# A four-layer transformer kernel: the activations' tiles start at other byte distances from the weight rings

## The chip, the cores and the metric

The kernel runs on one core of one Trainium2 chip. The metric is the time on the device in microseconds (us), here the median of three runs. Inside the core, TensorE (PE in the profile) multiplies; a matmul instruction streams its moving operand past a stationary operand that a weight load (PEld) has brought in before. VectorE (DVE), ScalarE (ACT) and GpSimd (POOL) do the work on elements, and SyncE (SP) issues DMA transfers.

## The reference

Activations are a 256 x 1024 matrix in float32. Two layers of a first block are followed by two layers of a second one. Cut to what matters:

```python
# first block, twice (layers 0 and 1)
h = rms_norm(x, mix_pre_norm[l])
m = hybrid_mixer(h, w_in[l], ...)          # delta rule, retention and pooling branches, gates, w_out
x = x + rms_norm(m, mix_post_norm[l])
h = rms_norm(x, ffn_pre_norm[l])
x = x + rms_norm(swiglu(h, ffn_gate[l], ffn_up[l], ffn_down[l]), ffn_post_norm[l])   # 1024 -> 2816 -> 1024

# second block, twice (layers 2 and 3)
u = rmsnorm(h, attn_norm[l])
h = h + hybrid_mixer_2(u, pos, w_in[l], ...)    # three attention branches, gates, w_o
u = rmsnorm(h, mlp_norm[l])
h = h + jnp.square(jax.nn.relu(u @ w_up[l])) @ w_down[l]                             # 1024 -> 4096 -> 1024
```

## The kernel before

**Weights.** All weight matrices are cut into 572 chunks of 128 partitions x 1024 float32. SP brings each chunk into one of four slots of `raw`; ACT rounds it into the ring `whi` (float32r, four slots), and DVE (for 54 chunks POOL) writes the remainder `raw - whi` into the ring `wlo`. A slot is 4096 bytes of each partition and a block of 128 columns in it is 512 bytes, so that every block of either ring starts at the same place modulo 512.

**Activations.** They are split in the same way. The normed stream is `hh` (high part, written by ACT in `high`) and `hl` (remainder, written by DVE in `low`, for the first pair of a turned norm by POOL), each 8 tiles of 256 tokens; a tile is 1024 bytes of each partition. The factor of the output projections is `FH` and `FL` (up to 32 tiles, 22 in layers 0 and 1, 32 in layers 2 and 3), which lie in slots 0 to 7 and 8 to 15 of the area. Each product is then three matmuls (`mm3`): high weights by high activations, high by low, low by high, summed in one bank.

**The order of the work.** Each engine's instructions are written out in program order by one function for each engine (`tensor` for PE). A layer has a mixer, where projections of the stream (`project`, `by_token`) and branches are interleaved with many small matmuls of the delta rule or of attention, and then long stretches of nothing but `mm3`:

- `gu` (layers 0 and 1) and `up` (layers 2 and 3): `project`, weights stationary, `hh` and `hl` moving, 256 columns a matmul;
- `down` of layers 2 and 3: `by_rows`, weights stationary, `FH` and `FL` moving, 256 columns a matmul;
- `wout` and `down` of layers 0 and 1: `tokens`, the other way round, `FH` and `FL` stationary, weights moving, 512 columns a matmul.

Before layer 0's and 1's delta rule there are also 16 matmuls of a small weight `SW`: for each of eight k, `SW[:, k, :]` (16 columns) is stationary under `hh[:, k, :]`, and then `SW[:, k, 0:8]` (8 columns) under `hl[:, k, :]`. `SW[:, k, :]` starts 64 bytes after `SW[:, k - 1, :]`.

**Where the tiles lie.** `sb` hands out addresses in the order of its calls, from byte 16640 of each partition. Worked out from the sizes: `whi` starts at 41216 and `wlo` at 57600, both 256 modulo 512. `hh` starts at 88000, `hl` at 96192, `SW` at 105408 and the area (`region`) at 105920, all 448 modulo 512. So `hh`, `hl`, `FH`, `FL` and the branches' factors (`B0H`, `B0L` and so on, in slots of the area) all start 192 bytes after a block of the rings, modulo 512. That is called the distance below. For the 16 matmuls of `SW` the moving tile starts -64 k bytes from the stationary one, modulo 512: at 0, 448, 384, 320, 256, 192, 128 and 64 for k from 0 to 7.

Of the kernel before, what the change touches and what calls it, by code (L numbers as in the profile page):

```python
# [14 lines left out]
P = 128  # L15
# [42 lines left out]
N_PAR = DEPTH * (N_PAR1 + N_PAR2)  # L58
N_SMALL = 64 + 512 + 8


# [132 lines left out]
def pair(t, j):  # L194
    return t[:, 512 * j:512 * j + 512]
# [76 lines left out]
def program(nc, ins, out):  # L272
    with ExitStack() as ctx:
# [63 lines left out]

        def slot_r(name, i, k):
            return sb(name, [P, k, T], F32R, offset=region + 4096 * i)

# [275 lines left out]
        def scalar(a):  # L616
# [47 lines left out]
            def high(norm, j, *ready):  # L664
                if norm in TURNED and j == 0:
                    a.wait_ge(*v_norm.at("first", norm))
                else:
                    a.wait_ge(*ready)
                for k in (2 * j, 2 * j + 1):
                    h = act(hh[:, k, :], xT[:, k, :], AF.Copy, scale=GAIN[norm][:, k:k + 1])  # L670
# [178 lines left out]
            def merge(name, L, j):  # L849

                a.wait_ge(*gated(name, L, 2 * j))
                act(FH[:, 2 * j:2 * j + 2, :], v3(pair(YY, j)), AF.Copy, scale=0.5).then_inc(*a_br.up("sum", L, j))

# [8 lines left out]
            def first(L):  # L862
# [68 lines left out]
                def product(i):  # L931
                    a.wait_ge(*v_ffn.at("product", L, i))
                    a.copy(FH[:, i, :], FT[:, 512 * (i % 4):512 * (i % 4) + T]).then_inc(*a_ffn.up("high", L, i))

# [30 lines left out]
            def second(L):  # L965
# [113 lines left out]
                def mlp_high(m0):  # L1079
                    f = FT[:, 256 * (m0 % 8):256 * (m0 % 8) + 512]  # L1080
                    a.wait_ge(*a_ffn.at("square", L, m0))
                    a.copy(FH[:, m0:m0 + 2, :], v3(f)).then_inc(*a_ffn.up("high", L, m0))

# [45 lines left out]
        def vector(v):  # L1129
# [52 lines left out]
            def low(norm, j):  # L1182
                v.wait_ge(*a_norm.at("high", norm, j))
                for k in (2 * j, 2 * j + 1):
                    x = stt(hl[:, k, :], xT[:, k, :], GAIN[norm][:, k:k + 1], hh[:, k, :].bitcast(F32), OP.mult, OP.subtract)
                x.then_inc(*v_norm.up("low", norm, j))
# [225 lines left out]
            def merge(L, j):  # L1412

                v.wait_ge(*a_br.at("sum", L, j))
                stt(FL[:, 2 * j:2 * j + 2, :], v3(pair(YY, j)), 0.5, FH[:, 2 * j:2 * j + 2, :].bitcast(F32), OP.mult, OP.subtract).then_inc(*v_br.up("merged", L, j))

# [8 lines left out]
            def first(L):  # L1425
# [104 lines left out]
                def ffn_low(i):  # L1530
                    v.wait_ge(*a_ffn.at("high", L, i))
                    tt(FL[:, i, :], f_(i)[:, 0:T], FH[:, i, :].bitcast(F32), OP.subtract).then_inc(*v_ffn.up("low", L, i))

# [53 lines left out]
            def second(L):  # L1587
# [162 lines left out]
                def mlp_low(m0):  # L1750
                    v.wait_ge(*a_ffn.at("high", L, m0))
                    tt(FL[:, m0:m0 + 2, :], v3(f_(m0)), FH[:, m0:m0 + 2, :].bitcast(F32), OP.subtract).then_inc(*v_ffn.up("low", L, m0))

# [31 lines left out]
        def gpsimd(g):  # L1785
# [28 lines left out]
            def low(norm):  # L1814

                g.wait_ge(*a_norm.at("high", norm, 0))
                for k in (0, 1):
                    x = g.tensor_scalar(SQ2[:, (6 + k) * T:(7 + k) * T], xT[:, k, :], GAIN[norm][:, k:k + 1], None, OP.mult)
                x.then_inc(*g_norm.up())
                g.wait_ge(*g_norm.now())  # L1820
                tt(hl[:, 0:2, :], v3(pair(SQ2, 3)), hh[:, 0:2, :].bitcast(F32), OP.subtract).then_inc(*g_norm.up("low", norm))

# [173 lines left out]
        def tensor(e):  # L1996
# [30 lines left out]
            def parts(job, ready, norm):  # L2027

                b, at = job.banks[0], job.first
                fresh(b, leaves(job.name, job.layer, 0))  # L2030
                for m in range(2):
                    e.wait_ge(*wlo_at(at + m))
                for k in range(8):
                    e.wait_ge(*(a_norm.at("high", norm, k // 2) if k else a_norm.at("first", norm)))
                    for m in range(2):
                        i = (at + m) % RING
                        mm(bank[b][:, m * T:(m + 1) * T], whi[:, i, 128 * k:128 * k + 128], hh[:, k, :], (m, k) == (0, 0), False, True)
                        mm(bank[b][:, m * T:(m + 1) * T], wlo[:, i, 128 * k:128 * k + 128], hh[:, k, :], False, False, True)
                for j in range(4):
                    e.wait_ge(*ready(j))  # L2040
                    for m in range(2):
                        for k in (2 * j, 2 * j + 1):
                            x = mm(bank[b][:, m * T:(m + 1) * T], whi[:, (at + m) % RING, 128 * k:128 * k + 128], hl[:, k, :], False, k == 7, True)
                        if j == 3:
                            x.then_inc(*proj.up("used", at + m, also=(job.name, job.layer, 0) if m else None))
# [61 lines left out]
            def by_token(name, L):  # L2107
                job = JOBS[name, L]
                for c in range(4):
                    i = job.first + c  # L2110
                    e.wait_ge(*wlo_at(i))
                    if c == 0:
                        for s in range(2):
                            fresh(job.banks[s], leaves(name, L, s))
                    for j in range(2):
                        k = 2 * c + j
                        wh, wl = whi[:, i % RING, 512 * j:512 * j + 512], wlo[:, i % RING, 512 * j:512 * j + 512]
                        for s in range(2):
                            ps = bank[job.banks[s]][:, :]
                            xh, xl = hh[:, k, 128 * s:128 * s + 128], hl[:, k, 128 * s:128 * s + 128]  # L2120
                            mm(ps, xh, wh, k == 0, False)
                            mm(ps, xl, wh, False, False)
                            x = mm(ps, xh, wl, False, k == 7)
                            if j == 1 and c == 3:
                                x.then_inc(*proj.up(name, L, s, also=("used", i) if s else None))
                            elif j == 1 and s == 1:
                                x.then_inc(*proj.up("used", i))
                    yield

            def tokens(name, L, ready, norm, then):  # L2130
# [6 lines left out]
                def term(k, b):  # L2137
                    i, s, f = job.first + k, 128 * (b // 2), 512 * (b % 2)
                    wh, wl = whi[:, i % RING, f:f + 512], wlo[:, i % RING, f:f + 512]
                    xh, xl = FH[:, k, s:s + 128], FL[:, k, s:s + 128]  # L2140
                    mm(bank[b][:, :], xh, wh, k == 0, False, True)
# [29 lines left out]
            def by_rows(name, L, ready, after=None):  # L2171
# [299 lines left out]
            def first(L):  # L2471
                norm = f"mixpre{L}"
                h = hh, hl, stream_ready(norm)

# [12 lines left out]
                for k in range(8):  # L2487
                    mm(bank[1][0:16, 0:T], SW[:, k, :], hh[:, k, :], k == 0, False, True)
                    x = mm(bank[1][0:8, 0:T], SW[:, k, 0:8], hl[:, k, :], False, k == 7, True)
                x.then_inc(*e_dn.up("abrow", L))  # L2490
# [24 lines left out]
                norm = f"ffnpre{L}"  # L2515
                rest(project("gu", L, hh, hl, stream_ready(norm), lambda: norm_sum(norm), norm=norm))
                tokens("down", L, lambda k: v_ffn.at("low", L, k), f"ffnpost{L}", "mixpre1" if L == 0 else "attn2")

            def second(L):
                norm = f"attn{L}"  # L2520
                h = hh, hl, stream_ready(norm)

# [78 lines left out]
                norm = f"mlp{L}"  # L2601
                rest(project("up", L, hh, hl, stream_ready(norm), lambda: norm_sum(norm)))
                by_rows("down", L, lambda k: v_ffn.at("low", L, k // 2 * 2), post("last") if L == 3 else None)
# [243 lines left out]
```

## Time and profile before

| | us |
|---|---|
| median of three runs | 1875.36 |
| lowest and highest of them | 1869.99, 1878.12 |
| span of the profiled execution | 1875.1 |
| PE busy in it | 1841.3 (98%), 15964 matmuls |
| DVE, ACT, POOL busy | 1259.6, 956.6, 307.3 |
| HBM read | 305.00 MB, 163 GB/s over the span |

Matmuls are pipelined: the profile gives each its own length of some 0.28 us, while the next one starts some 0.11 us after it. How fast PE gets through a stretch is therefore read from the starts, or from the chain of waits, which gives a stretch's time and its count of instructions. The profile's clock row gives the TensorE clock granted in tenths of full speed (2.4 GHz).

### The profile page before, as it was taken

What the parts mean: (1) busy time and instruction counts of PE and PEld (TensorE: products, weight loads), DVE (VectorE), ACT (ScalarE), POOL (GpSimd) and SP (SyncE); (2) the same over time, 40 slices, a digit from 0 to 9 for tenths busy, and PEclk for the clock granted to TensorE, in tenths of its full rate; (3) what the DMA queues carried; (4) which work ended last, traced back from release to release, by engine and by line L of the source; (5) the groups of instructions that cost most, each with busy time, mean ns of one, the idle gap of its engine ahead of it and who ended that gap; (6) DMA issues with size and microseconds to landing.
All of it is one profiled execution on the core that took longest, in us unless ns stands there. A gap on an engine that the chain in (4) does not pass through costs nothing.

```text
span 1875.1 us, 37406 instructions
## 1 busy us (share of the span) xinstructions
PE 1841.3 (98%) x15964; PEld 1750.7 (93%) x15964; DVE 1259.6 (67%) x1676; ACT 956.6 (51%) x1381; POOL 307.3 (16%) x176
## 2 busy tenths in 40 slices
PE   7999999999999999999999999999999999999998
PEld 7989998998888999999989999999999899999998
DVE  6884677665689557777648865676547785577643
ACT  5634466444563445554545455565434445555533
POOL 0050221000003212200002542310002352230000
PEclk9999999999999999999999999999999999999999
DMA  6443354656445334555656553456555663446652
GB/s 238 157 159 113 125 169 158 214 184 196 154 145 172 113 123 149 178 194 181 204 189 196 193 170 126 147 182 198 185 189 181 206 195 126 136 158 203 189 187 96
DMA packets 92165, 317.66 MB, mean 169 GB/s; under 512 B 11744, under 2 KB 12896, under 8 KB 91744
## 3 DMA queue, kind: packets, MB, share of 16 engines
q1 hardware_dynamic: 91424, 314.69, 51.7%
q8 instruction: 127, 2.08, 0.5%
q10 hardware_dynamic: 576, 0.57, 0.1%
q14 instruction: 38, 0.31, 0.0%
HBM read 305.00 MB, written 1.05 MB: 163 GB/s over the span
## 4 chain that ended last, share of the span: by engine, by line
PE 83%; DVE 12%; ACT 3%; issue 1%; DMA 1%; SPq 0%; DVEq 0%; ACTq 0%
PE bank L2007 82%; DVE wlo L1131 4%; DVE area L1131 3%; DVE area L1137 2%; ACT area L634 1%; ACT whi L640 1%; PE bank L2571 1%; DMA raw<-in_weights 1%; DVE hl L1137 1%; DVE xT L1137 1%; DVE area L1651 0%; DVE area L1649 0%; PE bank L2592 0%; ACT L622 0%; PE bank L2226 0%
## 5 line engine op out<-in xcount | busy, mean ns | idle before, releaser
L1131 DVE TENSOR_TENSOR wlo<-raw,whi 128x1024 fp32r<-128x1024 f32 x518 | 668.6, 1305 | 412.6 <-ACT whi L640 412.3
L2007 PE MATMUL bank<-hh,whi 128*128 128x256 f32 x2928 | 830.0, 284 | 18.5 <-DVE wlo L1131 15.9
L2007 PE MATMUL bank<-hh,wlo 128*128 128x256 f32 x2928 | 814.4, 279 | 0.0
L2007 PE MATMUL bank<-hl,whi 128*128 128x256 f32 x2928 | 807.2, 279 | 0.0
L640 ACT CAST whi<-raw 128x1024 fp32r<-128x1024 f32 x572 | 589.3, 1046 | 398.8 <-PE bank L2007 351.9
L2007 PEld LDWEIGHTS bank<-hh,whi 128*128 128x128 f32 x2928 | 551.3, 188 | 33.8 <-DVE wlo L1131 18.7
L2007 PEld LDWEIGHTS bank<-hl,whi 128*128 128x128 f32 x2928 | 551.1, 190 | 1.4 <-issue 1.4
L2007 PEld LDWEIGHTS bank<-hh,wlo 128*128 128x128 f32 x2928 | 551.4, 188 | 0.0
L1787 POOL TENSOR_TENSOR area<-area 128x512 f32<-128x512 f32 (+4 forms) x86 | 135.1, 1578 | 567.3 <-DVE area L1137 250.6
L1787 POOL TENSOR_TENSOR wlo<-raw,whi 128x1024 fp32r<-128x1024 f32 x54 | 133.9, 2481 | 384.7 <-ACT whi L640 384.7
L2007 PE MATMUL bank<-FH,whi 128*128 128x256 f32 x640 | 180.1, 281 | 0.0
L2007 PE MATMUL bank<-FL,whi 128*128 128x256 f32 x640 | 179.6, 281 | 0.0
L2007 PE MATMUL bank<-FH,wlo 128*128 128x256 f32 x640 | 179.6, 281 | 0.0
L634 ACT ACTIVATE area<-area 128x256 f32<-128x256 f32 (+8 forms) x247 | 140.8, 579 | 45.2 <-DVE area L1137 15.2
L2007 PE MATMUL bank<-area 128*64 128x64 f32 (+6 forms) x2464 | 154.7, 248 | 5.4 <-DVE area L1131 4.7
L2007 PEld LDWEIGHTS bank<-area 128*64 128x64 f32 (+3 forms) x2464 | 133.2, 151 | 24.2 <-issue 6.5
L2007 PEld LDWEIGHTS bank<-FL,whi 128*128 128x128 f32 x640 | 122.3, 191 | 0.1
L2007 PEld LDWEIGHTS bank<-FH,whi 128*128 128x128 f32 x640 | 120.1, 188 | 0.4 <-issue 0.3
L2007 PEld LDWEIGHTS bank<-FH,wlo 128*128 128x128 f32 x640 | 120.5, 188 | 0.0
L1131 DVE TENSOR_TENSOR area<-bank,RSB 128x512 f32<-128x512 f32 (+1 forms) x118 | 80.1, 681 | 37.9 <-PE bank L2007 36.1
L1131 DVE TENSOR_TENSOR area<-bank,area 128x512 f32<-128x512 f32 (+3 forms) x144 | 83.0, 616 | 23.7 <-PE bank L2007 23.3
L2007 PE MATMUL bank<-wlo,FH 128*128 128x512 f32 x240 | 94.9, 395 | 0.0
(132 smaller groups left out, 1907.4 us busy)
## 6 DMA issues: line engine op xcount, KB each, us to landing
raw<-in_weights SPq DMA_DIRECT2D x572, 512.0 KB, 4.0
area<-area SPq DMA_DIRECT2D x96, 64.0 KB, 3.6
area<-area SPq DMA_DIRECT2D x16, 128.0 KB, 3.9
cst<-in_const SPq DMA_DIRECT2D x1, 1188.0 KB, 7.9
cst<-in_const SPq DMA_DIRECT2D x1, 1024.5 KB, 5.6
xT<-in_x SPq DMA_DIRECT2D x4, 256.0 KB, 7.9
out<-xT SPq DMA_DIRECT2D x4, 256.0 KB, 2.9
area<-in_lev SPq DMA_DIRECT2D x2, 384.0 KB, 6.8
```

Of the source, the lines that this page charges most:

```text
L634: return a.activation(dst, src, fn, scale=scale, **more)
L640: a.copy(whi[:, i % RING, :], raw[:, i % RAW, :]).then_inc(*hi.up(i))
L1131: return v.tensor_tensor(dst, x, y, op)
L1137: return v.scalar_tensor_tensor(out=dst, in0=x, scalar=s, in1=y, op0=op0, op1=op1)
L1787: return g.tensor_tensor(dst, x, y, op)
L2007: return e.matmul(ps, x, y, start=start, stop=stop, skip_group_check=skip)
L2571: o = e.transpose(bank[b][:, 128 * u:128 * u + 128], x.grid()[:, j % 2, j // 2, 128 * kb:128 * kb + 128], C("eye"))
```

## The change

The tiles `hh` and `hl` become one pair for each layer, all in the same two places but for a shift under 512 bytes; `FH` and `FL` likewise. The shift sets the distance from a block of the rings to 64, 128, 448 and 224 bytes for the stream of layers 0 to 3, and to 320, 448, 256 and 384 bytes for the factors. All other tiles keep theirs: `RSB`, `SW`, the area and all that lies in it move up by exactly 512 bytes. Each use picks its layer's pair. No instruction is added, removed or moved on any engine, no size changes, and no wait.

For the 16 matmuls of `SW` the distance changes too, since `hh` and `hl` move and `SW` doesn't.

```diff
+STREAM_PHASE = (64, 128, 448, 224)
+
+FACTOR_PHASE = (320, 448, 256, 384)
...
+        whi_at = at[0]
         whi = sb("whi", [P, RING, 1024], F32R)
...
-        hh = sb("hh", [P, 8, T], F32R)
-        hl = sb("hl", [P, 8, T], F32R)
+        stream = at[0]
+        at[0] += 2 * 4 * 8 * T + 512
...
-        def slot_r(name, i, k):
-            return sb(name, [P, k, T], F32R, offset=region + 4096 * i)
+        def slot_r(name, i, k, behind=0):
+            return sb(name, [P, k, T], F32R, offset=region + 4096 * i + behind)
+
+        def from_weights(first, by):
+            return (whi_at + by - first) % 512
+
+        hh, hl = ([sb(f"{name}{L}", [P, 8, T], F32R, offset=stream + 8192 * j + from_weights(stream, STREAM_PHASE[L]))
+                   for L in range(2 * DEPTH)] for j, name in enumerate(("hh", "hl")))
...
-        FH, FL = slot_r("FH", 0, 32), slot_r("FL", 8, 32)
+        FH, FL = ([slot_r(f"{name}{L}", i, 32, from_weights(region, FACTOR_PHASE[L])) for L in range(2 * DEPTH)]
+                  for name, i in (("FH", 0), ("FL", 8)))
...
-                        mm(bank[b][:, m * T:(m + 1) * T], whi[:, i, 128 * k:128 * k + 128], hh[:, k, :], (m, k) == (0, 0), False, True)
+                        mm(bank[b][:, m * T:(m + 1) * T], whi[:, i, 128 * k:128 * k + 128], hh[job.layer][:, k, :], (m, k) == (0, 0), False, True)
...
-                    return mm3(bank[m // 2][:, m % 2 * T:m % 2 * T + T], job.first + k, 128 * m, FH[:, k, :], FL[:, k, :],
+                    return mm3(bank[m // 2][:, m % 2 * T:m % 2 * T + T], job.first + k, 128 * m, FH[L][:, k, :], FL[L][:, k, :],
```

## Rows read from the trace of the kernel before

**Rows 1.** The page: busy time, share and instructions of each engine; granted clock in 40 slices.

```profile
PE 1841.3 (98%) x15964; PEld 1750.7 (93%) x15964; DVE 1259.6 (67%) x1676; ACT 956.6 (51%) x1381; POOL 307.3 (16%) x176
...
PEclk9999999999999999999999999999999999999999
```

**Rows 2.** Chain of waits in seven stretches, 256-column matmuls: start us, us, what, count.

```profile
320.00 110.09 PE bank L2007 x935
...
808.93 39.23 PE bank L2007 x333
...
864.92 54.17 PE bank L2007 x478
...
1252.92 77.11 PE bank L2007 x655
...
1332.97 90.10 PE bank L2007 x765
...
1694.00 76.08 PE bank L2007 x646
...
1774.91 80.21 PE bank L2007 x681
```

**Rows 3.** Groups by shape, PE and PEld, 320 to 430 us: count, busy us, mean ns.

```profile
L2007 PE MATMUL bank<-hl,whi 128*128 128x256 f32 x311 | 87.4, 281 | 0.0
...
L2007 PEld LDWEIGHTS bank<-hl,whi 128*128 128x128 f32 x310 | 59.5, 192 | 0.0
L2007 PEld LDWEIGHTS bank<-hh,whi 128*128 128x128 f32 x311 | 58.4, 188 | 0.0
```

**Rows 4.** The same view, 866 to 918 us.

```profile
L2007 PE MATMUL bank<-hl,whi 128*128 128x256 f32 x154 | 42.5, 276 | 0.0
...
L2007 PEld LDWEIGHTS bank<-hl,whi 128*128 128x128 f32 x153 | 28.7, 188 | 0.0
```

**Rows 5.** Timeline of PE around one interruption: start us, us, engine, what.

```profile
862.49 0.28 PE L2007 MATMUL bank<-hh,wlo 128*128 128x256 f32 x1
862.60 0.37 PE L2007 MATMUL bank<-hh,whi 128*128 128x256 f32 x1
862.81 0.28 PE L2007 MATMUL bank<-hl,whi 128*128 128x256 f32 x1
```

**Rows 6.** Timeline of PE, matmuls of SW, layer 0, k = 1 to 4.

```profile
24.15 0.28 PE L2007 MATMUL bank<-hh,SW 128*16 128x256 f32 x1
24.26 0.28 PE L2007 MATMUL bank<-hl,SW 128*8 128x256 f32 x1
24.38 0.28 PE L2007 MATMUL bank<-hh,SW 128*16 128x256 f32 x1
24.50 0.28 PE L2007 MATMUL bank<-hl,SW 128*8 128x256 f32 x1
24.61 0.28 PE L2007 MATMUL bank<-hh,SW 128*16 128x256 f32 x1
24.73 0.28 PE L2007 MATMUL bank<-hl,SW 128*8 128x256 f32 x1
```

**Rows 7.** The same of layer 1, k = 1 and 2.

```profile
512.10 0.28 PE L2007 MATMUL bank<-hh,SW 128*16 128x256 f32 x1
512.21 0.28 PE L2007 MATMUL bank<-hl,SW 128*8 128x256 f32 x1
512.33 0.28 PE L2007 MATMUL bank<-hh,SW 128*16 128x256 f32 x1
512.45 0.28 PE L2007 MATMUL bank<-hl,SW 128*8 128x256 f32 x1
```

**Rows 8.** Chain of waits in `down` of layers 0 and 1, 512-column matmuls.

```profile
433.97 60.20 PE bank L2007 x258
...
920.91 59.53 PE bank L2007 x260
```

**Rows 9.** Groups by shape, PE, in the mixers (12-282, 500-770, 985-1227, 1423-1668 us).

```profile
L2007 PE MATMUL bank<-hl,whi 128*128 128x256 f32 x445 | 124.0, 279 | 0.0
...
L2007 PE MATMUL bank<-hl,whi 128*128 128x256 f32 x448 | 121.8, 277 | 0.0
...
L2007 PE MATMUL bank<-hl,whi 128*128 128x256 f32 x408 | 111.0, 278 | 0.0
...
L2007 PE MATMUL bank<-hl,whi 128*128 128x256 f32 x408 | 113.7, 279 | 0.0
```

**Rows 10.** The page: costliest groups (count, busy us, mean ns, idle before).

```profile
L1131 DVE TENSOR_TENSOR wlo<-raw,whi 128x1024 fp32r<-128x1024 f32 x518 | 668.6, 1305 | 412.6 <-ACT whi L640 412.3
...
L640 ACT CAST whi<-raw 128x1024 fp32r<-128x1024 f32 x572 | 589.3, 1046 | 398.8 <-PE bank L2007 351.9
```

More of the change, by code:

```diff
@@ L669, in high @@
                 for k in (2 * j, 2 * j + 1):
-                    h = act(hh[:, k, :], xT[:, k, :], AF.Copy, scale=GAIN[norm][:, k:k + 1])
+                    h = act(hh[int(norm[-1])][:, k, :], xT[:, k, :], AF.Copy, scale=GAIN[norm][:, k:k + 1])
                     if norm in TURNED and k == 0:
@@ L851, in merge @@
                 a.wait_ge(*gated(name, L, 2 * j))
-                act(FH[:, 2 * j:2 * j + 2, :], v3(pair(YY, j)), AF.Copy, scale=0.5).then_inc(*a_br.up("sum", L, j))
+                act(FH[L][:, 2 * j:2 * j + 2, :], v3(pair(YY, j)), AF.Copy, scale=0.5).then_inc(*a_br.up("sum", L, j))
             def by_rows(name, L, settle={}):
@@ L932, in product @@
                     a.wait_ge(*v_ffn.at("product", L, i))
-                    a.copy(FH[:, i, :], FT[:, 512 * (i % 4):512 * (i % 4) + T]).then_inc(*a_ffn.up("high", L, i))
+                    a.copy(FH[L][:, i, :], FT[:, 512 * (i % 4):512 * (i % 4) + T]).then_inc(*a_ffn.up("high", L, i))
                 def ffn(m0):
@@ L1081, in mlp_high @@
                     a.wait_ge(*a_ffn.at("square", L, m0))
-                    a.copy(FH[:, m0:m0 + 2, :], v3(f)).then_inc(*a_ffn.up("high", L, m0))
+                    a.copy(FH[L][:, m0:m0 + 2, :], v3(f)).then_inc(*a_ffn.up("high", L, m0))
                 def mlp(m0):
@@ L2036, in parts @@
                         i = (at + m) % RING
-                        mm(bank[b][:, m * T:(m + 1) * T], whi[:, i, 128 * k:128 * k + 128], hh[:, k, :], (m, k) == (0, 0), False, True)
-                        mm(bank[b][:, m * T:(m + 1) * T], wlo[:, i, 128 * k:128 * k + 128], hh[:, k, :], False, False, True)
+                        mm(bank[b][:, m * T:(m + 1) * T], whi[:, i, 128 * k:128 * k + 128], hh[job.layer][:, k, :], (m, k) == (0, 0), False, True)
+                        mm(bank[b][:, m * T:(m + 1) * T], wlo[:, i, 128 * k:128 * k + 128], hh[job.layer][:, k, :], False, False, True)
                 for j in range(4):
@@ L2042, in parts @@
                         for k in (2 * j, 2 * j + 1):
-                            x = mm(bank[b][:, m * T:(m + 1) * T], whi[:, (at + m) % RING, 128 * k:128 * k + 128], hl[:, k, :], False, k == 7, True)
+                            x = mm(bank[b][:, m * T:(m + 1) * T], whi[:, (at + m) % RING, 128 * k:128 * k + 128], hl[job.layer][:, k, :], False, k == 7, True)
                         if j == 3:
@@ L2139, in term @@
                     wh, wl = whi[:, i % RING, f:f + 512], wlo[:, i % RING, f:f + 512]
-                    xh, xl = FH[:, k, s:s + 128], FL[:, k, s:s + 128]
+                    xh, xl = FH[L][:, k, s:s + 128], FL[L][:, k, s:s + 128]
                     mm(bank[b][:, :], xh, wh, k == 0, False, True)
@@ L2472, in first @@
                 norm = f"mixpre{L}"
-                h = hh, hl, stream_ready(norm)
+                h = hh[L], hl[L], stream_ready(norm)
                 def sums():
@@ L2487, in first @@
                 for k in range(8):
-                    mm(bank[1][0:16, 0:T], SW[:, k, :], hh[:, k, :], k == 0, False, True)
-                    x = mm(bank[1][0:8, 0:T], SW[:, k, 0:8], hl[:, k, :], False, k == 7, True)
+                    mm(bank[1][0:16, 0:T], SW[:, k, :], hh[L][:, k, :], k == 0, False, True)
+                    x = mm(bank[1][0:8, 0:T], SW[:, k, 0:8], hl[L][:, k, :], False, k == 7, True)
                 x.then_inc(*e_dn.up("abrow", L))
@@ L2520, in second @@
                 norm = f"attn{L}"
-                h = hh, hl, stream_ready(norm)
+                h = hh[L], hl[L], stream_ready(norm)
                 def key(m0):
```

16 lines of the change are left out of this document (8 added, 8 removed).

## The prediction

> **What bounds the kernel now.** I read the page's engine row first: PE is busy 98% of the span and the other engines 67% or less [rows 1]. The granted clock is 9 in all slices, so PE runs at 2.4 GHz throughout and the clock has nothing to give. Next I read the chain of waits. In the long stretches of `gu`, `up` and `down` it is one piece of PE matmuls after another [rows 2], so the kernel's end moves there by exactly as much as PE's pace does.
>
> The pace is what matters. Time over count, from the seven pieces [rows 2]: 110.09 / 935 = 117.7 ns, 39.23 / 333 = 117.8, 54.17 / 478 = 113.3, 77.11 / 655 = 117.7, 90.10 / 765 = 117.8, 76.08 / 646 = 117.8, 80.21 / 681 = 117.8. These are the same instructions with the same shapes, and they run at exactly two paces, 117.75 and 113.3 ns, 4% apart. The groups by shape tell the two apart as well: a matmul has a mean of 281 ns at the slow pace and 276 at the fast one, and the weight load for `hl` takes 192 ns at the slow pace and 188 at the fast one, where that for `hh` takes 188 at both [rows 3, 4]. Streaming 256 columns at 2.4 GHz is 106.7 ns, so both paces carry something on top.
>
> The pace doesn't drift inside a stretch. The `gu` of layer 1 runs slowly, meets interruptions (one is seen where a matmul takes 0.37 us and the next starts 0.21 us after it instead of 0.11 [rows 5]), and runs fast from there on to its end. So a pace looks like one of two stable patterns between the weight load that reads one tile and the matmul that reads another at the same time, and an entry into a stretch picks the pattern.
>
> Does an address enter into it? The matmuls of `SW` say yes. There only the stationary address moves, by 64 bytes each k, and the distances between starts for k = 1, 2 and 3 are 0.11, 0.12, 0.12, 0.11 and 0.12 us [rows 6]. In layer 1, 488 us later, the first three differences are again 0.11, 0.12 and 0.12 [rows 7]. Had this been noise the two layers wouldn't agree; the pattern repeats where addresses and instructions repeat. These loads bring only 16 or 8 columns, so they are a far row for the change, but they are the only ones of the trace at another distance than 192.
>
> **The change part by part.** It adds no instruction, no wait and no byte moved. Its sum has the pace as its only kind of term.
>
> *Stream, long stretches* (`gu` at 64 and 128 bytes, `up` at 448 and 224). Now slow: 935 + 333 + 655 + 646 = 2569 matmuls [rows 2]. At the fast pace each is 4.4 ns shorter, 11.3 us together. Now fast: 478, which would lose 2.1 us at the slow pace.
>
> *Factors, long stretches* (`down` of layers 2 and 3, at 256 and 384 bytes). Slow: 765 + 681 = 1446 [rows 2], worth 6.4 us. None of it is fast today, so nothing is at risk but a third pace.
>
> *Factors as the stationary operand* (`down` of layers 0 and 1, 512 columns). 60.20 / 258 = 233.3 ns against 59.53 / 260 = 229.0 [rows 8]: two paces again, 4.3 ns apart. Layer 0 can gain 258 x 4.3 = 1.1 us, and layer 1 can lose as much.
>
> *Mixers.* The mean of the `hl` matmuls is 277 to 279 ns [rows 9], between 276 and 281, so both paces occur. Means take in restarts like that of 0.37 us, which is why I take only a third as slow. Counted as three times the `hl` rows there are 3 x 1709 = 5127 matmuls: some 1700 slow and 3400 fast. Here waits for DVE and ACT stand between short pieces of PE, and a gain that falls in front of one is lost; I let 0.7 of it through, an estimate between none and all. All fast: -1700 x 4.4 x 0.7 = -5.2 us. All slow: +3400 x 4.4 x 0.7 = +10.5. The branches' own tiles keep their 192 bytes. I enter the mixers at zero, with both ends kept for the range.
>
> *What a faster PE meets next.* A chunk of weights is 24 matmuls, 2.72 us at the fast pace. DVE needs 1.305 us for its remainder and ACT 1.046 us for its rounding [rows 10], so the supply stays ahead, as it does in the fast stretch of layer 1 that is one unbroken piece of PE [rows 2].
>
> *What the tiles' writers pay.* ACT, DVE and POOL write `hh`, `hl`, `FH` and `FL` in the same shapes. The trace shows none of their instructions at another alignment, so I bound this cost by what such a writer takes of the path in the long stretches, none. Zero it is.
>
> The sum for the likeliest outcome: all six slow stretches go to the fast pace, 11.3 + 6.4 = 17.7, layer 0's `down` 1.1, together -18.8 us; mixers 0. The profiled span is 1875.1, 0.3 under the median of the runs, so 1875.4 - 18.8 = 1856.6, say **1856**.
>
> Why the fast pace rather than a fresh draw at the same odds? Six of seven long pieces sit at the slow pace today [rows 2], all at 192 bytes, while the `SW` matmuls show both intervals within a few steps of 64 bytes. A place that is unlucky six times out of seven has far more room above it than below, and a move to any other place is likelier to leave that than to keep it. This is the weakest step of the argument: a switch of places could also leave some of the stretches where they are.
>
> **A rule that speaks against it.** What rows show: two weight loads of the same size read at the same time as a matmul take 192 and 188 ns [rows 3], so the reads seem to disturb each other. The Trainium skill says otherwise in "TensorE: Matmul & The Clock Gate", section "Step-by-step: what each phase is for": TensorE has two independent read ports, and loading the next weights takes nothing from the running matmul. "SBUF — State Buffer", section "Who interferes with whom", adds that PE and ACT never wait on anyone. By that rule the distance is without meaning and the change is worth nothing.
>
> **The rivals.**
>
> *Nothing happens (0.10).* Both paces come from something else, such as the sequence of waits at an entry, which the change leaves as it is. For it: the interruption that changed the pace moved no address [rows 5]. Against it: `SW`. It gives the time of before, 1875. It is also what the skill's rule gives.
>
> *Only some stretches turn (0.22).* An entry decides each stretch anew, and three of six turn, as `gu` of layer 1 shows both paces in one layer [rows 2]. Half of 18.8 is -9.4 us: 1866, with about half of this case on each side of the 0.5% bound.
>
> *The fast stretches are the ones that turn (0.16).* At 64 and 128 bytes the reads of the stream of layers 0 and 1 meet more, not less: `gu` of layer 1 loses 2.1 us, its `down` 1.1, and the mixers up to 10.5, while the long slow stretches stay. That is +13.7 us, 1889. It ends slower than before from +9.4 us on, that is, when some 2100 matmuls on the chain go from fast to slow with none coming back; the mixers have to go nearly as a whole. Against it: so many fast pieces would have to be hit while none of the slow ones is.
>
> *A third, lower pace (0.05).* At a distance where the reads never meet, less than 113.3 ns would be possible; the bound from below is 106.7. No row of 256 columns shows it, `SW` with its tiny loads included, whose shortest interval is 0.11 us. If the 2569 + 478 + 1446 = 4493 matmuls of the long stretches came halfway, to 110 ns, that is another 4493 x 3.3 = 14.8 us on top: 1842. The Trainium skill's "Back-to-back issue gap" in "TensorE: Matmul & The Clock Gate" would put a lone matmul of 256 columns at 109.2 ns; no long stretch here comes near it.
>
> **How the numbers follow.** The forecast has 0.47, part of the stretches 0.22, nothing 0.10, the other side 0.16, the lower pace 0.05. A measurement of this kernel can tell about 0.5% (9.4 us) from no change. Faster by more: 0.47 + 0.05 + half of 0.22 less a hundredth = 0.62. Within: 0.10 + 0.12 = 0.22. Slower: 0.16. The range begins at 1856 with the mixers' 5.2 gained too and some of the lower pace, 1845, and reaches up over the partial case and no change with the spread of its runs (to 1878.1) and the nearer part of the slow side, to 1884. Outside are most of the 0.16 and of the 0.05. The forecast's own range is 1845 to 1865.
>
> **What would show it right or wrong.** In the trace of the changed kernel the seven pieces of the chain [rows 2] have to come out at 113.3 ns a matmul, the `hl` matmul's mean at 276 and its weight load at 188 ns [rows 3] in all of them. `down` of layer 0 has to be at 229 [rows 8]. The `SW` intervals should change their pattern, since their distances do: if they stay, the address has no part in it and the forecast is wrong from its root. A mixer's `hl` mean over 279 [rows 9] speaks for the slow rival, a pace between or above the two for a pattern I haven't seen. Wrong would also be that stretches turn fast and the span doesn't follow; then something other than PE is next, which rows 10 would show as DVE or ACT waits.

## The result and the profile after

The changed kernel takes 1891.2 us (median of four runs, 1886.6 to 1893.3) against 1876.0 for the kernel before. The ratio is 1.0084 with an interval of 1.0062 to 1.0106: slower by 0.8%, where 1856 us was forecast and 1884 was the end of the range.

The page of the changed kernel, engines and clock. TensorE is as busy as before and its clock is full; nothing new stands in its way. It does the same 15964 matmuls and takes 15 us longer over them [rows 1].

```profile
span 1890.1 us, 37406 instructions
PE 1862.3 (99%) x15964; PEld 1771.4 (94%) x15964; DVE 1252.3 (66%) x1676; ACT 957.0 (51%) x1381; POOL 307.8 (16%) x176
...
PEclk9999999999999999999999999999999999999999
```

The chain of waits of the changed kernel in the long stretches, `gu` of layer 0, the two parts of `gu` of layer 1, `up` and `down` of layer 2, and the same of layer 3 (start us, us, what, count):

```profile
324.97 110.12 PE bank L2020 x935
...
811.92 43.16 PE bank L2020 x364
...
863.96 64.08 PE bank L2020 x534
...
1264.98 76.08 PE bank L2020 x646
...
1345.00 90.12 PE bank L2020 x751
...
1699.95 87.12 PE bank L2020 x736
...
1791.92 80.10 PE bank L2020 x675
```

Time over count, beside [rows 2]: 117.8 ns (117.7 before), 118.6 (117.8), 120.0 (113.3), 117.8 (117.7), 120.0 (117.8), 118.4 (117.8) and 118.7 (117.8). No long stretch runs at 113.3 ns any more, and two paces are there that the trace of before didn't have: about 118.5, and 120.0.

In the mixers the mean of the `hl` matmuls went from 279, 277, 278 and 279 ns [rows 9] to 282, 282, 278 and 281:

```profile
L2020 PE MATMUL bank<-hl,whi 128*128 128x256 f32 x444 | 125.1, 282 | 0.0
...
L2020 PE MATMUL bank<-hl,whi 128*128 128x256 f32 x448 | 123.7, 282 | 0.0
...
L2020 PE MATMUL bank<-hl,whi 128*128 128x256 f32 x408 | 111.1, 278 | 0.0
...
L2020 PE MATMUL bank<-hl,whi 128*128 128x256 f32 x408 | 114.6, 281 | 0.0
```

The only mixer that kept its mean is that of layer 2, whose stream lies at 448 bytes.

To see where the 15 us lie I cut both traces at the first and last matmul of each use of the factors and took the differences of the starts. Stage times in us, before and after:

```
             before    after
mixers 0-3   272.4 274.8 239.3 236.5    275.8 276.4 239.8 238.4    +7.4
gu, up       130.0 128.4  91.0  91.0    130.2 132.2  90.9  91.5    +4.4
wout, wo      21.7  21.7  22.4  22.4     22.2  21.7  22.9  22.7    +1.2
down          61.4  60.2  90.3  92.4     61.4  60.2  92.0  93.1    +2.4
```

The matmuls of `SW` bear on the distance too. In layer 1 their distances are 448, 384, 320 and so on down to 0, one step of k behind those of before. Timeline of PE in the changed kernel, from 320 bytes (k = 2) on:

```profile
516.29 0.28 PE L2020 MATMUL bank<-hh,SW 128*16 128x256 f32 x1
516.41 0.28 PE L2020 MATMUL bank<-hl,SW 128*8 128x256 f32 x1
516.52 0.28 PE L2020 MATMUL bank<-hh,SW 128*16 128x256 f32 x1
516.63 0.28 PE L2020 MATMUL bank<-hl,SW 128*8 128x256 f32 x1
516.75 0.28 PE L2020 MATMUL bank<-hh,SW 128*16 128x256 f32 x1
```

In nanoseconds the nine intervals from there are 114, 113, 115, 118, 117, 116, 117, 116, 118. In the kernel before, counted from the same distance and so from k = 3, the third pair of [rows 6], they are 114, 113, 115, 118, 117, 116, 117, 116, 118. In this trace the pattern has gone with the distance, to the nanosecond. In layer 0 of the changed kernel the six intervals from k = 4 on are 117, 116, 117, 116, 118, 116, the same as in its layer 1 from k = 4 on, though the distances are 64 bytes lower there (128 against 192): what came before counts too. These rows are a weak witness all the same. The run with the stream alone moved has the same distances in layer 1 and takes the intervals 114, 119, 116, 120, 117, 116, 117, 116, 118 from k = 2 on; the run with everything back at 192 has the distances of before and takes 113, 114, 113, 113, 114 in layer 0 where the kernel before took 113, 119, 117, 113, 114.

### The profile page after: what moved, and what is told of

Read it like the earlier page. It is cut to its first block, busy times and chain, and to the rows that moved or that the text cites. A ratio compares the mean times of both kernels' runs of the same rounds, so it can differ in the third digit from the quotient of the medians.

```text
span 1890.1 us, 37406 instructions
## 1 busy us (share of the span) xinstructions
PE 1862.3 (99%) x15964; PEld 1771.4 (94%) x15964; DVE 1252.3 (66%) x1676; ACT 957.0 (51%) x1381; POOL 307.8 (16%) x176
## 4 chain that ended last, share of the span: by engine, by line
PE 85%; DVE 10%; ACT 3%; issue 1%; DMA 1%; SPq 0%; DVEq 0%; ACTq 0%
PE bank L2020 84%; DVE wlo L1144 3%; DVE area L1144 3%; DVE area L1150 2%; ACT area L647 1%; ACT whi L653 1%; PE bank L2584 1%; DMA raw<-in_weights 1%; DVE hl L1150 1%; DVE xT L1150 1%; PE bank L2605 0%; PE bank L2239 0%; DVE area L1214 0%; DVE xT L1144 0%; ACT L635 0%
## 5 line engine op out<-in xcount | busy, mean ns | idle before, releaser
L1144 DVE TENSOR_TENSOR wlo<-raw,whi 128x1024 fp32r<-128x1024 f32 x518 | 661.1, 1291 | 418.4 <-ACT whi L653 418.0
L2020 PE MATMUL bank<-whi,FL 128*128 128x512 f32 x240 | 94.6, 394 | 0.0
```

The source lines that it names most:

```text
L1144: return v.tensor_tensor(dst, x, y, op)
L2020: return e.matmul(ps, x, y, start=start, stop=stop, skip_group_check=skip)
```

## The experiments

The theory after the result, A: the distance in bytes between the moving tile and the stationary one sets which paces a stretch of matmuls can take, and the way it is entered picks one of them. Rivals: B, each entry draws its pace whatever the address; C, the 512 bytes by which the area moved, or the new layout as such, cost the time. Each run below is compared with runs of the kernel before on the same chip. Paces are time over count of the chain's pieces.

**All distances back at 192**

```diff
-STREAM_PHASE = (64, 128, 448, 224)
+STREAM_PHASE = (192, 192, 192, 192)
-FACTOR_PHASE = (320, 448, 256, 384)
+FACTOR_PHASE = (192, 192, 192, 192)
```

> The changed kernel with every distance set back to 192 bytes; only the 512 bytes by which RSB, SW and the area moved up are left of the change. Theory A (pace follows from the distance between moving and stationary tile, and repeats from run to run): the kernel before in all but name, ratio 1.000 within 0.003, gu of layer 0 at 117.8 ns a matmul, second part of gu of layer 1 at 113.3, down of layers 2 and 3 at 117.8, the same SW intervals as before. Theory B (each entry draws a pace, whatever the address): other stretches slow than before, a span anywhere from 1856 to 1895 us. Theory C (the move of the area by 512 bytes or the other layout costs): 1891, as after the change.

1875.65 us, ratio 1.0006 (0.9991 to 1.0022). The chain's pieces of `gu` of layer 0, the end of `gu` of layer 1, and `down` of layer 2:

```profile
321.93 112.12 PE bank L2020 x952
...
865.90 56.22 PE bank L2020 x493
...
1334.89 90.22 PE bank L2020 x766
```

They are 117.8, 114.0 (a short slow part at its head) and 117.8 ns, as before. C has fallen. B has nearly fallen: `up` and `down` of layers 2 and 3 came out within 0.1 us of before. One long piece didn't: the first part of `gu` of layer 1 behind the norm's sum, at 117.8 ns before, ran at 113.3 here. So the entry differs between executions of one set of distances.

**The stream alone, and the factors alone**

```diff
 STREAM_PHASE = (64, 128, 448, 224)
-FACTOR_PHASE = (320, 448, 256, 384)
+FACTOR_PHASE = (192, 192, 192, 192)
```

> Stream distances as changed (64, 128, 448, 224), factors all at 192. Theory A: the mixers and gu of layers 0 to 3 as slow as after the change, some +7 us in the mixers and +4 us in gu of layer 1, so 1886 to 1889 us, while down of layers 2 and 3 stays at 117.8 ns as before. If the factors' distances are the cause: 1878 us at most.

1884.4 us, ratio 1.0050 (1.0031 to 1.0068).

```diff
-STREAM_PHASE = (64, 128, 448, 224)
+STREAM_PHASE = (192, 192, 192, 192)
 FACTOR_PHASE = (320, 448, 256, 384)
```

> Factor distances as changed (320, 448, 256, 384), stream all at 192. Theory A: mixers and gu as before; down of layer 2 at 120.0 ns (+1.7 us), down of layer 3 at 118.7 (+0.7), wo +0.7 together, so 1878 to 1880 us. If the factors were the main cause: above 1885.

1881.5 us, ratio 1.0048 (1.0026 to 1.0071). So each half costs about as much, and the two together (0.98%) cost no less than the change (0.84%). With the stream alone, `down` of layers 2 and 3 kept its 90.34 and 92.36 us; the mixers cost +7.1 us and `gu` of layer 1 +3.0. With the factors alone `down` of layer 2 takes 92.02 us. What I hadn't expected is `up` of layer 2, whose distance is that of before. The chain's pieces of `up` and then `down` of layer 2 in that trace:

```profile
1258.96 73.10 PE bank L2020 x645
...
1334.93 95.06 PE bank L2020 x794
```

`up` of layer 2 runs at 113.3 ns here and at 117.7 in [rows 2], at the same 192 bytes, while `down` behind it, at 256, is at 119.7 with its edges. The stretch was entered differently: ahead of the norm's sum its pace was 117.8 ns here and 113.3 in the trace of before. That the factors' distance did this is likely, but one trace shows it. Both halves of the theory, distance and entry, are needed.

**A map of the distances**

One run had stream and factors at 0, five more had two distances each, one in layers 0 and 2 and one in layers 1 and 3; the stream and the factors of a layer had the same. The edit is the two tuples alone, such as

```diff
-STREAM_PHASE = (64, 128, 448, 224)
+STREAM_PHASE = (256, 320, 256, 320)
-FACTOR_PHASE = (320, 448, 256, 384)
+FACTOR_PHASE = (256, 320, 256, 320)
```

> All distances 0: moving and stationary tiles start at the same place modulo 512. Theory A says that a new distance gives a new set of paces, each on one of the levels 113.3, 117.8 and 120.0 ns, the same in like layers; I can't say which. Theory B: a mixture no different from that at 192. Between 1860 and 1900 us either way; what decides is whether layers 0 and 1 agree with each other, and 2 and 3.

> Stream and factors at 256 bytes in layers 0 and 2, at 320 in layers 1 and 3. Theory A (the distance sets which paces a stretch can take, the entry picks among them): down of layer 2 at 120.0 ns again, as in the changed kernel that had 256 there; gu of layer 0 and up of layer 2 alike with each other, between 117.8 and 120.0. For 320, seen so far only with the roles turned round (which is 192): one of 113.3 to 120.0, the same in gu of layer 1, up and down of layer 3. Theory B' (0 is the one bad place, all others are a draw between 113.3 and 117.8): down of layer 2 would not come back to 120.0 by itself.

> 384 bytes in layers 0 and 2, 448 in layers 1 and 3. Theory A: 448 has both 113.3 and 117.8 ns, as the stream of layer 2 in the changed kernel; 384 has 118.7 to 120.0 in down of layer 2, as layer 3's factors there. Theory B': no order.

> 64 bytes in layers 0 and 2, 128 in layers 1 and 3. Theory A: gu and mixer of layer 0 at 117.8 ns and of layer 1 at 118.7 to 120.0, as in the changed kernel with the same two distances; layers 2 and 3 follow with the same values. If the two blocks differ at the same distance, the entry counts for more than the distance.

> 224 bytes in layers 0 and 2, 160 in layers 1 and 3: 32 bytes to either side of the 192 of before. Theory A in its coarse form (only steps of 64 bytes count): one of them behaves as 192 (113.3 in the mixers, 117.8 in the long stretches). In its fine form each has paces of its own; 224 has 118.3 in the mixer and up of layer 3 of the changed kernel, so layers 0 and 2 should be there.

> 32 bytes in layers 0 and 2, 96 in layers 1 and 3. Theory A in its fine form, from what 160 and 224 gave: each has paces between its neighbours', 32 some 118 to 120 and 96 some 117.8 to 118.7, with no 113.3 in a long stretch; some 1893 us.

The medians are 1901.7 us (0), 1896.7 (256 and 320), 1887.2 (384 and 448), 1894.2 (64 and 128), 1894.3 (224 and 160) and 1896.0 (32 and 96, one time only). The chain's pieces, one for each distance: in the run at 0 `gu` of layer 0; at 256 and at 64 `down` of layer 2 and `gu` of layer 0; at 128 `gu` of layer 1; at 224 and 160 `gu` of layers 0 and 1; at 32 `down` of layer 2 and at 96 `up` of layer 3.

```profile
322.99 112.08 PE bank L2020 x934
...
1349.99 90.12 PE bank L2020 x751
...
325.00 110.00 PE bank L2020 x934
...
866.96 58.15 PE bank L2020 x490
...
324.97 110.05 PE bank L2020 x930
...
867.90 57.14 PE bank L2020 x487
...
1344.96 85.05 PE bank L2020 x729
...
1699.92 85.16 PE bank L2020 x710
```

Worked out for the long stretches, with what the others of the same runs add:

| distance | 256 columns, weights stationary, ns | 512 columns, factors stationary, ns |
|---|---|---|
| 0, 256 | 120.0 | 226.7 |
| 32 | 116.7 | 233.3 |
| 64, 320 | 117.8 | 233.3 |
| 96 | 120.0 | 234.2 |
| 128, 384 | 118.7 or 120.0 | 232.4 |
| 160 | 117.3 to 118.8 | 233.4 |
| 192, 448 | 113.3 or 117.8 | 228.9 or 233.3 |
| 224 | 118.3 | 233.3 |

(For the second column the tiles' distance is the same number, the roles of moving and stationary are exchanged.) In the long stretches no distance but 192 and 448 has the fast pace at all. A step of 32 bytes is enough to lose it there. In shorter pieces it isn't theirs alone. In the run with the stream alone moved, layer 0's stream lies at 64, and the 96 matmuls of its `gu` ahead of the norm's sum run at 113.3 ns (fifteen intervals in 1.70 us):

```profile
321.58 0.28 PE L2020 MATMUL bank<-hh,wlo 128*128 128x256 f32 x1
...
323.28 0.28 PE L2020 MATMUL bank<-hh,wlo 128*128 128x256 f32 x1
```

Behind the sum the pace was 117.8. In the six other `gu` and `up` stretches at 64 or 320 it was 117.8 on both sides of the sum. At 32, too, pieces of 96 and 168 matmuls ran at another pace, 117.8, than the long stretches. So the map says which paces last in a long stretch, and not all that can occur.

One thing the map leaves open. The rings start at the same place modulo 512 in every run, so the distance and the moving tile's own place in the partition are the same number but for a constant. Only the matmuls of `SW`, whose stationary tile moves, tell the two apart, and they are the weak witness above.

At 0 everything is slow in the same way, in both blocks and at every entry. Groups by shape of the run at 0, 330 to 430 us:

```profile
L2020 PEld LDWEIGHTS bank<-hh,whi 128*128 128x128 f32 x279 | 53.6, 192 | 0.0
L2020 PEld LDWEIGHTS bank<-hl,whi 128*128 128x128 f32 x278 | 53.4, 192 | 0.0
L2020 PEld LDWEIGHTS bank<-hh,wlo 128*128 128x128 f32 x278 | 53.4, 192 | 0.0
```

All three loads take 192 ns. At 192 bytes' slow pace it was one of the three [rows 3], and at its fast pace none [rows 4]. But a load's length is no measure of the pace in general: in `gu` of layer 0 of the changed kernel, at 64 bytes and the same slow 117.8 ns, all three take 188 ns or less (330 to 420 us), and in its `down` of layer 2, at 120.0 ns, 189.

```profile
L2020 PEld LDWEIGHTS bank<-hl,whi 128*128 128x128 f32 x256 | 48.1, 188 | 0.0
```

**All distances at 448**

```diff
+STREAM_PHASE = (448, 448, 448, 448)
+FACTOR_PHASE = (448, 448, 448, 448)
```

> All distances 448 bytes. The table so far has 0 like 256, 64 like 320, 128 like 384, 192 like 448. If the paces repeat every 256 bytes (theory A with a period of 256): the kernel before again, 113.3 and 117.8 ns and nothing else, no stretch at 118.3 or 120, 1875 us within 5. If the period is 512: other paces, in down of layers 2 and 3 above all, and 1885 or more.

1870.6 us, ratio 0.9989 (0.9955 to 1.0023). The pieces of `gu` of layer 0, of the end of `gu` of layer 1 and of `down` of layer 2, as in the first run:

```profile
322.00 110.00 PE bank L2020 x934
...
864.91 55.20 PE bank L2020 x485
...
1334.99 90.10 PE bank L2020 x765
```

117.8, 113.8 and 117.8 ns; stage by stage all of `gu`, `up`, `down` and `wout` are within 0.02 us of before. The paces of 192 repeat 256 bytes on, and in the map those of 0, 64 and 128 do too. The change's 448 for the stream of layer 2 was therefore as good as no move, which fits the mean that this mixer kept.

**What picks the pace at 192**

In the traces at 192 or 448 bytes the pace after the norm's sum, which stands 96 matmuls inside `gu` and `up`, was always the other one of 113.3 and 117.8 ns than ahead of it. Over all runs, the later ones too, these are 41 stretches in 13 traces: 37 turned from fast to slow and four from slow to fast. Two runs changed this sum, in `gu` and `up` of the kernel before:

```diff
-                for c in (0, 128):
+                for c in (0, 128) * (2 if norm[:3] in ("ffn", "mlp") else 1):
                     x = mm(bank[b][:, c:c + 128], C("ones"), SQ2[:, c:c + 128], True, True)
```

> The kernel before, all distances 192; the two matmuls of the norm's sum that stand inside gu and up are issued twice over, with the same result. In the traces so far the pace always turns to the other one of 113.3 and 117.8 ns across this pair of matmuls. Theory E (at 192 two patterns are stable, and the pair turns one into the other): the long rest of gu of layer 0 (957 matmuls), up of layers 2 and 3 (672 each) and down of layers 2 and 3 behind them may come to 113.3; -4.3, -3.0 and -3.0 us in the first three, less 0.4 us for each of four doubled pairs, so 1866 us, and 1860 if down follows. Rival (the pace is drawn by the length of the wait before the pair): no piece, or any, changes, and 1877 us is as likely as less.

```diff
-                for c in (0, 128):
-                    x = mm(bank[b][:, c:c + 128], C("ones"), SQ2[:, c:c + 128], True, True)
+                w = T if norm[:3] in ("ffn", "mlp") else 128
+                for c in range(0, T, w):
+                    x = mm(bank[b][:, c:c + w], C("ones"), SQ2[:, c:c + w], True, True)
```

> As the run before, but the sum is taken by one matmul of 256 columns in the place of two of 128, in gu and up only. Theory E leaves open whether one wide matmul turns the pattern: if it does, the paces and the time of before, 1875; if it does not, 113.3 ns in the three long rests and 1865. Between these there is nothing but gu of layer 1, whose entry varies.

1874.1 and 1879.8 us against 1873.2, ratios 1.0001 (0.9970 to 1.0031) and 1.0030 (1.0008 to 1.0052). Neither gave what theory E hoped for. (The profiled execution with the wide matmul spans 1874.1 us and was the fastest of its ten; its trace shows no cause for the 0.3% of its ratio.) Issued twice, the pair turned the pace once, just as the single pair does; so did the wide matmul. `gu` of layer 0 came to the doubled pair at 117.8 ns in this execution and left it at the fast pace:

```profile
322.89 107.21 PE bank L2007 x946
```

113.3 ns over 946 matmuls, against 117.7 in [rows 2]; the stage took 126.39 us instead of 130.00. What turns the pace is then, it seems, the break that such matmuls make in the sequence of triples, whether they are one, two or four. A break by a wait doesn't always do it, as is seen further below in `gu` of layer 1. The next run adds a second break, of matmuls that nobody uses, two steps later. Its wait is over by then: the added pair starts 0.12 us after the matmul ahead of it.

```diff
                     if hook and step == 2:
                         hook()
+                    if name in ("gu", "up") and step == 4:
+                        e.wait_ge(*a_norm.at("log", {"gu": "ffnpre", "up": "mlp"}[name] + str(L)))
+                        for c in (0, 128):
+                            mm(bank[0][:, c:c + 128], C("ones"), C("ones"), True, True)
```

> The kernel before with two more matmuls of 128 columns (ones by ones, into a bank that nobody reads then) two steps after the norm's sum in gu and up; nothing else. In eleven traces at 192 or 448 bytes the pace after the norm's sum was the other one than ahead of it, whether the pair was issued once, twice or as one wide matmul. Theory F (any such break in the stream of triples turns 113.3 into 117.8 ns and back): one more turn brings the long rest of gu of layer 0 and up of layers 2 and 3, slow before, to 113.3, about -4, -2.8 and -2.8 us, and down of layers 2 and 3 may follow; 1866 us or less. Rival (the norm's sum turns it by its own operands or wait): the added pair leaves the pace as it is or sets it at random; 1877 us.

1866.6 us against 1877.3, ratio 0.9944 (0.9920 to 0.9967): 16 short matmul entries more in the trace, and 10 us less. (The kernel before had medians of 1869.9 and 1871.5 us in two other sets of runs on this chip, so the size of the gain is less sure than its sign.) The timeline around the added pair in `gu` of layer 0:

```profile
325.85 0.28 PE L2007 MATMUL bank<-hl,whi 128*128 128x256 f32 x1
325.97 0.28 PE L2007 MATMUL bank<-hh,wlo 128*128 128x256 f32 x1
326.09 0.61 PE L2007 MATMUL bank<-cst 128*128 128x128 f32 x4
326.45 0.37 PE L2007 MATMUL bank<-hh,whi 128*128 128x256 f32 x1
```

The chain's pieces behind it, in `gu` of layer 0, `up` and `down` of layer 2, `up` and `down` of layer 3:

```profile
326.94 103.14 PE bank L2007 x910
...
1256.96 70.05 PE bank L2007 x618
...
1327.92 86.13 PE bank L2007 x760
...
1690.90 68.11 PE bank L2007 x601
...
1760.94 82.75 PE bank L2007 x730
```

All five are at 113.3 or 113.4 ns; in [rows 2] they were at 117.7 and 117.8. `down` inherits the pace of `up`. The profiled span is 1859.5 us, 15.6 under that of before; the medians differ by less. This execution was the second fastest of eight; that others enter a stretch the other way is likely, but no trace of them is kept.

**The change with the same second break**

> The changed kernel (64, 128, 448, 224 and 320, 448, 256, 384) with the same added turn. Theory F with the table of distances: only 192 and 448 have two patterns to turn between, so up of layer 2 (448) comes to 113.3 ns, -2.3 us, and gu of layers 0 and 1 and up of layer 3 stay at 117.8, 118.7 or more, and 118.3, each 0.4 us longer by the pair: 1890 us. If a turn helped at any distance, it would be 1880 or less.

1891.2 us, ratio 1.0102 (1.0062 to 1.0141): no gain. `gu` of layer 0, at 64 bytes, stays at 104.12 / 884 = 117.8 ns behind the added pair. `up` of layer 2, at 448, was turned twice, but had been entered slowly and so ended at 117.8: the part between the two breaks ran at 113.3 (first row), the rest did not (second row). My -2.3 us for it was wrong for that reason, and the rest of the expectation held.

```profile
1264.40 4.65 PE bank L2020 x41
...
1270.89 70.20 PE bank L2020 x596
```

So the break that helps at 192 doesn't give the change its loss back: in `gu` of layers 0 and 1 and `up` of layer 3 the distance allowed no fast pace behind it.

**Do the stages add up?**

```diff
+STREAM_PHASE = (192, 192, 192, 192)
+FACTOR_PHASE = (0, 0, 32, 32)
```

> Stream at 192 everywhere, factors at 0 in layers 0 and 1 and at 32 in layers 2 and 3. If the table of paces holds stage by stage: wout and down of layers 0 and 1, with the factors stationary under 512 columns, at 226.7 ns as in the run with all at 0 (-1.7, -0.6 and twice -0.2 us), down of layers 2 and 3 at 116.7 as in the run with 32 and 96 (-0.9 us each): 1871 us against 1875.4, a difference at the edge of what the rounds can tell; the stage times in the trace decide. If stages do not add up (an entry upsets the next one): up of layer 2 or 3 changes pace though its distance does not.

1869.7 us against 1877.3, ratio 0.9960 (0.9942 to 0.9978). `down` of layers 0 and 1 took 59.64 and 59.63 us, that of layers 2 and 3 89.49 and 91.60, `wout` 21.55 twice, all within 0.1 us of the map. The `up` stretches kept their pace. Then both edits together, with the factors of layers 2 and 3 back at 192:

> The added turn in gu and up together with factors at 0 in layers 0 and 1; stream and the other factors at 192. If the two gains add: the stages of the run with the turn alone, with wout and down of layers 0 and 1 at 21.55 and 59.64 us instead of 21.74 and 60.20, 1.5 us more, a span of 1858 and a ratio of 0.993. If the entries upset each other, a long rest is back at 117.8 ns and 3 to 4 us are lost.

1862.1 us against 1871.5, ratio 0.9946 (0.9922 to 0.9971). The stages of the factors came as expected, the long rests of `gu` of layer 0 and of `up` and `down` were fast, but the last part of `gu` of layer 1 fell to the slow pace (63.13 us for 536 matmuls, 117.8 ns) and gave 2.3 us back. By the ratios it is no better than the turn alone. Both beat the kernel before and the changed one.

**Which read disturbs which**

```diff
-        hh, hl = (... offset=stream + 8192 * j + from_weights(stream, STREAM_PHASE[L]))
+        hh, hl = (... offset=stream + 8192 * j + from_weights(stream, (192, 0)[j]))
```

> All at 192 but hl, which starts at 0; the factors stay at 192. A triple is whi under hh, whi under hl, wlo under hh. Theory G (a matmul is held up by the weight load that reads beside it, by their own distance): one of three matmuls is at the place of 120.0 ns and two at that of 113.3 or 117.8: a mean between, 115.6 to 118.5 ns in gu and up, and in the groups by shape one of the three weight loads is longer than the others. Rival (the triple locks as a whole): 113.3, 117.8 or 120.0 as a whole again.

1889.7 us (one time). In `gu` of layer 0 the pace is 104.11 / 873 = 119.3 ns, above what theory G gave. It is no steady pattern either: the sums of three neighbouring intervals wander between 349 and 363 ns, where at 192 each long stretch stays within a nanosecond of one value, and no weight load stands out, all three have a mean of 188 ns. So a triple with two distances is neither the sum of its matmuls nor one locked whole. `down` of layers 2 and 3 behind it, with all its tiles at 192, was entered the other way than before and ran at 113.3 ns (86.9 and 89.1 us), which hides 6.7 us of the loss in the total. How the two reads meet in detail stays open.

## Why the prediction was wrong, point by point

**What bounds the kernel: right.** PE's pace, and nothing else, carries the difference; no wait and no engine took its place. The two paces, their 4.4 ns, the chain's pieces and the 192 against 188 ns of the weight load were read rightly, and the address does enter. One reading was wrong: [rows 5] isn't where `gu` of layer 1 turned. The timeline of before shows 117.7 ns up to 850.69 us (30 intervals in 3.53 us) and 113.3 from soon after the wait that follows (30 in 3.40); the wait at 857.04 and the interruption at 862.60 [rows 5] left the pace as it was.

```profile
847.16 0.28 PE L2007 MATMUL bank<-hh,wlo 128*128 128x256 f32 x1
...
850.69 0.28 PE L2007 MATMUL bank<-hh,wlo 128*128 128x256 f32 x1
851.10 0.39 PE L2007 MATMUL bank<-hh,whi 128*128 128x256 f32 x1
...
853.15 0.28 PE L2007 MATMUL bank<-hh,wlo 128*128 128x256 f32 x1
...
856.55 0.28 PE L2007 MATMUL bank<-hh,wlo 128*128 128x256 f32 x1
857.04 0.39 PE L2007 MATMUL bank<-hh,whi 128*128 128x256 f32 x1 [0.22 <-DVE wlo L1131]
```

**The step that failed** is the one I had called the weakest: that 192 was an unlucky place, as six of seven pieces were slow there [rows 2], and that "a move to any other place is likelier to leave that than to keep it". The runs showed the reverse. 192 and 448 are the only distances of the map at which 113.3 ns occurs in the long stretches, so a move could at best keep it, at 448, and else lose it: all seven pieces came out at 117.8 to 120.0 ns. Six of seven pieces were slow because of how they were entered: five of them ran at 113.3 or 113.4 ns at the same 192 bytes once a second break had turned the pace. The distance says what is possible, the entry what happens, and I charged the second to the first. The rows held a warning: layer 1's `gu` went from slow to fast with no address moved [rows 2], which a place alone can't do, and the mixers showed the fast pace often [rows 9].

**Stream, long stretches.** Forecast -11.3 us for the slow parts, with 2.1 at risk. Measured +4.4: at 64 the slow pace stayed, at 128 the fast part of layer 1 went to 120.0 ns, at 224 the pace rose to some 118.4. The risk was too small because I took 117.8 ns for the worst; the map has 120.0.

**Factors.** Forecast -6.4 and -1.1; measured +2.4 in `down` of layers 2 and 3, nothing in that of layers 0 and 1, and +1.2 in `wout` and `wo`, for which I had no term.

**Mixers.** I entered zero between -5.2 and +10.5; it was +7.4, half of the whole loss. The end of the range was well placed, the entry wasn't: the three layers whose distance changed lost 6.9 of it, and the `hl` mean rose in these three alone.

**Writers and supply: right.** ACT's busy time is 957.0 us against 956.6, DVE's fell from 1259.6 to 1252.3, and neither comes to stand on the chain.

**The rivals.** "The fast stretches are the ones that turn" had 0.16 and gave 1889 us. Its way is what happened, but that the total fits to within 2 us is luck. It gave the mixers 10.5 us (measured 7.4), `gu` of layer 1 2.1 (3.8) and its `down` 1.1 (nothing), and it had nothing for the factors, which cost 3.6; and of the long slow stretches, which were to stay, some got slower still. A third pace was a rival too, but only below 113.3; it exists above. The rule that I took from the Trainium skill ("TensorE: Matmul & The Clock Gate", section "Step-by-step: what each phase is for"), that loading the next weights takes nothing from the running matmul, would leave the place of the tiles without meaning. The measurements differ from that: stream and factors at 0 and the same at 192 differ in nothing but the place of these tiles, and the first takes 26 us more (1901.7 against 1875.7).

**The signs to look for.** The intervals of `SW` were to change with their distances, and did, but the sign was worth less than I thought: for k = 1 to 3 they also differ between two traces at the same distances, as shown above. The weight load for `hl` was to be at 188 ns where the pace is fast; in `gu` of layer 0 it is at 188 and the pace is slow. `down` of layer 0 was to come to 229 ns and stayed at 233.3. Had I read those rows by distance instead of only for whether they vary, they would still not have given the long stretches' paces, since at 192 (k = 5) they show 117 and 116 ns, neither of its two.

## What to carry to other kernels

In a dense stream of float32r matmuls, the place of the moving tile against the stationary one, in bytes modulo 256, was worth up to 6% of the pace here; measure it as time over count in the chain, at steps of 32 bytes, and don't take the pace of one stretch for the property of its place. If the same instructions run at two paces, ask what the stretch came through: a short break in the stream can be cheaper than the slow pattern that it ends. And when a tuned number is moved, count what the present value already has, not only what it lacks.

## What the runs showed of the hardware

- With stream and factors at one distance in a layer, the mean interval between matmuls of 256 columns takes only a few values in the long stretches (113.3, 116.7, 117.3, 117.8, 118.3, some 118.7, 120.0 ns at 2.4 GHz). Which of them depends on the tiles' place with a period of 256 bytes: all at 448 gave the paces of all at 192, and the layers at 256 had the `gu`, `up` and `down` times of all at 0 (132.4, 92.7 and 92.0 us in both).
- At 192 and 448 two patterns are stable for hundreds of matmuls. A break of a few short matmuls turned one into the other each time that the traces show it (41 times by the norm's sum, nine times by the added pair). A wait can turn it or leave it: in `gu` of layer 1 the one ahead of 851.10 us did, the one ahead of 857.04 didn't. `up` hands its pattern on to `down` where both are at 192 or 448.
- With the roles exchanged and 512 columns moving, the best distance is another one: 226.7 ns at 0 against 228.9 or 233.3 at 192. Its chain's piece in `down` of layer 0, in the run with the factors at 0 there:

```profile
434.91 58.49 PE bank L2020 x258
```

- Since an entry through a wait can go either way, single times of the kernel before lie between 1856 and 1882 us. That this spread comes from the patterns is likely, as turning `up` and `down` of one layer is worth nearly 6 us, but no run separates it from other causes.
